# Gate and branch products of a second transformer block computed with tokens on the partitions, with a rearranged merge

## What is computed

```
h = rms_norm(x); z = h @ w_in
zq, zf_f, zf_b, zi, zg, zu, zv, ga, gb = split(z)
a_out = hgrn2_mixer(zq, zf_f, zf_b, zi, zg, ...)      # (256, 1024): two directions, 8 heads of 128
b_out = spatial_gating(zu, zv, ...)                   # (256, 512)
merged = sigmoid(ga) * (a_out @ w_a) + sigmoid(gb) * (b_out @ w_b)
x = x + rms_norm(merged @ w_out)
x = x + rms_norm((silu(h2 @ w_gate) * (h2 @ w_up)) @ w_down)      # h2 = rms_norm(x)
x = x + (p @ w_ple) * sigmoid(x @ w_ple_gate)
```

## Time and profile before

| | |
|---|---|
| three runs | 1087.6, 1088.25, 1090.77 us; median 1088.25 |
| profiled execution | 1089.45 us, its span (first to last instruction) 1087.7 us |
| PE busy | 1074.7 us, 99% of the span |
| DVE, ACT busy | 751.3 us (69%), 602.7 us (55%) |
| HBM read | 180.79 MB, 167 GB/s over the span |
| TensorE clock granted | full throughout |

### The profile page before, as it was taken

One profiled execution on the slowest core, in us unless ns is written; L12 is line 12 of the kernel. 1 busy time (PEld: TensorE's weight loads), 2 busy tenths in 40 slices (PEclk: granted clock), 3 DMA queues, 4 the chain that ended last, 5 costly groups with the idle time before them and its releaser, 6 DMA issues.

```text
span 1087.7 us, 16240 instructions
## 1 busy us (share of the span) xinstructions
PE 1074.7 (99%) x6880; PEld 960.4 (88%) x6880; DVE 751.3 (69%) x897; ACT 602.7 (55%) x731; POOL 0.2 (0%) x4
## 2 busy tenths in 40 slices
PE   9999999999999999999999999999999999999998
PEld 8888777789998988888889899999999888888887
DVE  5465855466745478776568897679947888776557
ACT  5543365543535455555446985589555675554443
POOL 0000000000000000000000000000000000000000
PEclk9999999999999999999999999999999999999999
DMA  9963244565553556564655455443544646664651
GB/s 281 244 215 117 78 155 145 149 209 186 169 188 117 155 184 215 191 194 146 212 182 180 133 156 166 144 156 117 155 155 146 193 155 195 193 194 155 196 172 39
DMA packets 141448, 183.08 MB, mean 168 GB/s; under 512 B 14132, under 2 KB 91936, under 8 KB 141376
## 3 DMA queue, kind: packets, MB, share of 16 engines
q1 hardware_dynamic: 141160, 181.85, 52.8%
q10 hardware_dynamic: 216, 0.21, 0.1%
HBM read 180.79 MB, written 1.25 MB: 167 GB/s over the span
## 4 chain that ended last, share of the span: by engine, by line
PE 91%; ACT 4%; DVE 3%; issue 1%; DVEq 0%; ACTq 0%
PE ps L543 28%; PE ps L569 22%; PE ps L600 14%; PE ps L571 11%; PE ps L987 2%; PE ps L1116 2%; PE ps L646 1%; DVE wlo L1753 1%; PE ps L806 1%; ACT whi L1169 1%; PE ps L781 1%; PE ps L648 1%; PE ps L793 1%; PE ps L876 1%; PE ps L1002 1%
## 5 line engine op out<-in xcount | busy, mean ns | idle before, releaser
L1753 DVE TENSOR_TENSOR wlo<-raw,whi 128x2048 fp32r<-128x2048 f32 (+3 forms) x170 | 378.4, 2228 | 173.1 <-ACT whi L1169 172.6
L1169 ACT ACTIVATE whi<-raw 128x2048 fp32r<-128x2048 f32 (+1 forms) x167 | 310.5, 1863 | 89.9 <-PE ps L571 36.2
L543 PE MATMUL ps<-ha,whi 128*128 128x256 f32 x1328 | 243.1, 285 | 4.3 <-DVE wlo L1753 4.3
L569 PE MATMUL ps<-ha,whi 128*128 128x512 f32 x640 | 226.2, 399 | 0.6 <-DVE wlo L1753 0.6
L543 PEld LDWEIGHTS ps<-ha,whi 128*128 128x128 f32 x1328 | 206.9, 192 | 8.2 <-issue 7.1
L543 PE MATMUL ps<-ha,wlo 128*128 128x256 f32 x664 | 187.8, 283 | 0.0
L571 PE MATMUL ps<-ha,wlo 128*128 128x256 f32 x640 | 179.4, 280 | 0.0
L569 PEld LDWEIGHTS ps<-ha,whi 128*128 128x128 f32 x640 | 120.2, 188 | 30.6 <-issue 0.9
L543 PEld LDWEIGHTS ps<-ha,wlo 128*128 128x128 f32 x664 | 127.2, 192 | 0.0
L569 PE MATMUL ps<-pr,whi 128*128 128x512 f32 x352 | 124.5, 399 | 0.0
L571 PEld LDWEIGHTS ps<-ha,wlo 128*128 128x128 f32 x640 | 120.8, 189 | 0.1
(11 more groups left out here) (381 smaller groups left out, 1691.7 us busy)
## 6 DMA issues: line engine op xcount, KB each, us to landing
raw<-in_w_in SPq DMA_DIRECT2D x54, 1024.0 KB, 5.3
raw<-in_w_ffn_gate SPq DMA_DIRECT2D x11, 1024.0 KB, 5.1
raw<-in_w_ffn_up SPq DMA_DIRECT2D x11, 1024.0 KB, 5.2
raw<-in_w_gate SPq DMA_DIRECT2D x11, 1024.0 KB, 5.1
raw<-in_w_up SPq DMA_DIRECT2D x11, 1024.0 KB, 5.1
raw<-in_w_xkv SPq DMA_DIRECT2D x8, 1024.0 KB, 5.1
raw<-in_w_ffn_down SPq DMA_DIRECT2D x8, 1024.0 KB, 5.0
raw<-in_w_down SPq DMA_DIRECT2D x8, 1024.0 KB, 5.0
```

The source lines that it names most:

```text
L543: mm = e.matmul(ps[0:width, m * T:(m + 1) * T], a[:, kk, m * width:(m + 1) * width], b[:, off + k, :], start=k == 0 and j == 0 and m % 2 = ...
L569: e.matmul(banks[s][:, at_:at_ + 512], wh[:, kk, c], H[2][:, :, k, :], start=k == 0, stop=False, skip_group_check=True)
L1169: e.activation(h, r, ACT.Copy).then_inc(*hi_done.up(n))
L1753: e.tensor_tensor(l, r, h.bitcast(F32), ALU.subtract).then_inc(*lo_done.up(n))
```

## The change

- **Second run of the mixer**: gb0, gb1, wb0, wb1, ga0 and ga1 are computed by `unit_tm` (ten units), and so are the four units of wa0 and wa1. The gates and the merge then have tokens on the partitions.
- **Merge**: each half of `mtmp` is turned back by eight transposes on PE (`turn_merged2`), one group between the two token halves of wa1.1, the other inside `paired` behind its first step; `ml_hi` and `ml_lo` read the turned result in PSUM. On DVE `merged2(1, 0)` comes ahead of `ml_lo(0, 0)`. On ACT the conversion of wa1.1 moves between the two `ao` copies of the second run, and the conversion of wo1 ahead of `ml_hi(0, 0)`.
- **First run of the mixer**: everything on PE from S0 on stands one unit later (S0 behind zu's first unit), and the conversion of zu's first unit stands ahead of the logarithms on ACT and DVE; the slots are renumbered, and `tanh_q(1)` comes ahead of `mix_norm(0)`.
- **Norm behind w_out**: the square and fold of the third piece stand ahead of the conversion of the next unit.
- **Residual**: `add_normed` computes X of tile k+1 ahead of the low part of tile k, in both uses.
- **Start**: the conversion of sq's first unit stands ahead of `rs_tm("mem")`; the masks are loaded behind cc's fetches and converted behind the convolution's taps.

```diff
         fetch_for("fk")
-        e.dma_start(mk[:, :, :], d["c_masks"].rearrange("p (l n) -> p l n", l=7)).then_inc(s_mk, 16)
         fetch_for("fv")
...
-        fetch_for("svf", "sq", "cc", "cu", "cb")
+        fetch_for("svf", "sq", "cc")
+        e.dma_start(mk[:, :, :], d["c_masks"].rearrange("p (l n) -> p l n", l=7)).then_inc(s_mk, 16)
+        fetch_for("cu", "cb")
...
+        def unit_tm(name, i, H, s, free=None, ncol=512, K=8, off=0, ready=None, halves_=False, between=None):
...
             for t in range(2):
+                if t and halves_:
+                    mm.then_inc(*half_done.up((name, 0)))
+                if t and between is not None:
+                    between()
                 for kk in range(nk):
+                    if ready is not None and t == 0 and ready(k) != last_wait:
+                        last_wait = ready(k)
+                        e.wait_ge(*last_wait)
...
-        mixer(0, 1)
-        linear("zu", HA, 0, None, a_stat.on(("ln", "final")), lambda i: mixer(0, 2 + i))
+        linear("zu", HA, 0, None, a_stat.on(("ln", "final")), lambda i: mixer(0, 1 + i))
...
-        linear("gb0", HA, 0, None, a_mix.on(("sig", 1, 1)), lambda i: mixer(1, 1 + i))
...
-        linear("ga1", HA, 1, None, v_evac.on("wb1"), lambda i: mixer(1, 9 + i))
+        for g in range(2):
+            for i in range(2):
+                unit_tm(f"gb{g}", i, HA, g, None if i else (a_mix.on(("sig", 1, 1)), v_mix.on(("zg", 1)))[g])
+                mixer(1, 1 + 2 * g + i)
+        e.wait_ge(*v_split.on("bo"))
+        for g in range(2):
+            unit_tm(f"wb{g}", 0, BO, g, a_stat.on(("tanh", f"gb{g}")), K=4)
+            mixer(1, 5 + g)
+        for g in range(2):
+            for i in range(2):
+                unit_tm(f"ga{g}", i, HA, g, None if i else v_evac.on(f"wb{g}"))
+                mixer(1, 7 + 2 * g + i)
...
+        def turn_merged2(i):
+            e.wait_ge(*v_stat.on(("merged2", i, 1)))
+            for m in range(4):
+                for t_ in range(2):
+                    mm = e.transpose(banks[i][:, m * T + t_ * P:m * T + t_ * P + P],
+                                     mtmp[i][:, 2 * t_ + m // 2, (m % 2) * P:(m % 2) * P + P], ident[:, :])
+                if m % 2:
+                    mm.then_inc(*pe_turn.up(("ml", i, m // 2)))
...
+        unit_tm("wa0", 0, AO, 0, a_stat.on(("tanh", "ga0")), ready=ao_ready)
         mixer(1, 11)
+        unit_tm("wa1", 0, AO, 1, a_stat.on(("tanh", "ga1")), ready=ao_ready)
+        unit_tm("wa0", 1, AO, 0, ready=ao_ready, halves_=True)
+        unit_tm("wa1", 1, AO, 1, halves_=True, between=lambda: turn_merged2(0))
         paired(("wo0", "wo1"), ML, (2, 3), lambda k: v_split.on(("ml", k // 4, k % 4 // 2)),
+               (mix_taken(1, 8, 0), a_mix.on(("ln", 1, 1))), 2, lambda: turn_merged2(1))
...
+        hi(U["svf"][0][0] + 2)
         rs_tm("mem", m_tm, 20)
-        hi_for("svf")
+        hi(U["svf"][1][0] + 2)
...
+                if i == 1 and j == 0:
+                    hi(U["wa1"][1][0])
...
         hi(U["hq0"][1][0] + 2)
+        hi(U["zv"][0][0] + 2)
         half_logs(0, 0)
...
         merged2(0, 1)
+        merged2(1, 0)
         ml_lo(0, 0)
         lo(U["wa1"][1][0] + 2)
+        merged2(1, 1)
         ml_lo(0, 1)
-        merged2(1, 0)
-        merged2(1, 1)
...
+            def added(k):
+                normed(k)
+                e.wait_ge(*v_stat.on(("nh", name, k)))
+                e.tensor_tensor(X[:, k, :], X[:, k, :], nh[:, k, :], ALU.add)
+            added(0)
             for k in range(8):
                 if k < 7:
-                    normed(k + 1)
+                    added(k + 1)
                 e.wait_ge(*v_stat.on((split_name, k)))
...
```

More of the change, by code:

```diff
@@ L588, in both @@
                         between(2 * i + g)
-        def unit_tm(name, i, H, s, free=None, ncol=512, K=8, off=0):
+        def unit_tm(name, i, H, s, free=None, ncol=512, K=8, off=0, ready=None, halves_=False, between=None):
             n, k0, nk = U[name][i]
             wh, wl = weights(n)
+            last_wait = None
             if free is not None:
@@ L629, in column_sums, with paired @@
             mm.then_inc(*pe_sum.up(("sums", name)))
-        def paired(names, H, ss, ready, frees, step=1):
+        def paired(names, H, ss, ready, frees, step=1, middle=None):
             last_wait = None
@@ L651, in paired @@
                         mm.then_inc(*unit_done.up(("unit", n)))
+                if k0 == 0 and middle is not None:
+                    middle()
         def sums_and_ple(name, s, free, i, ps, ready, ple_free):
@@ L1032, in tensor @@
         unit_tm("zv", 1, HA, 3)
-        mixer(0, 1)
-        linear("zu", HA, 0, None, a_stat.on(("ln", "final")), lambda i: mixer(0, 2 + i))
+        linear("zu", HA, 0, None, a_stat.on(("ln", "final")), lambda i: mixer(0, 1 + i))
         for i in range(2):
             unit_tm(f"zi{i}", 0, HA, 1 - i, v_mix.on(("q", 0)) if i == 0 else a_evac.on("zu"))
+            mixer(0, 3 + 2 * i)
+            unit_tm(f"zi{i}", 1, HA, 1 - i)
             mixer(0, 4 + 2 * i)
[L1038 to L1043, removed]
+        linear("zg0", HA, 1, None, a_evac.on(("zi0", 1)), lambda i: mixer(0, 7 + i))
+        linear("hq1", HA, 0, None, a_evac.on(("zi1", 1)), lambda i: mixer(0, 9 + i))
+        unit("ff1", 0, HA, 1, None, v_mix.on(("zg", 0)))
         mixer(0, 11)
-        linear("ff1", HA, 1, None, v_mix.on(("zg", 0)))
+        unit("ff1", 1, HA, 1)
         unit("fb1", 0, HA, 0, None, v_mix.on(("q", 1)))
@@ L1066, in ao_ready @@
         def ao_ready(k):
             return v_split.on(("ao", k // 4, k % 4 // 2))
-        unit("wa0", 0, AO, 0, ao_ready, a_stat.on(("tanh", "ga0")))
+        def turn_merged2(i):
[6 more added lines that the diff above has]
+                    mm.then_inc(*pe_turn.up(("ml", i, m // 2)))
@@ L1082, in tensor @@
         mm.then_inc(*pe_turn.up("p"))
-        piece("wo2", ML, 1, None, v_evac.on(("wa", 1, 1)))
+        piece("wo2", ML, 1, None, v_split.on(("ml", 1, 1)))
         piece("wo3", ML, 2, None, v_evac.on(("mix", 0)), last=True)
@@ L1601, in tanh_zg @@
                 *a_mix.up(("tanh zg", i)))
-        slot(U["zg0"][0][0], 0, 8)
-        hi(U["zg0"][1][0] + 2)
-        mix_scores(0, 8)
+        for k, (u, _, _) in enumerate(U["zg0"]):
+            slot(u, 0, 7 + k)
         tanh_zg(0)
         hi(U["hq1"][0][0] + 2)
-        mix_norm(0)
+        mix_scores(0, 8)
         hi(U["hq1"][1][0] + 2)
@@ L1659, in ml_hi @@
             k0 = 4 * i + 2 * j
-            e.wait_ge(*v_stat.on(("merged2", i, j)))
-            e.activation(ML[0][:, k0:k0 + 2, :], mtmp[i][:, 2 * j:2 * j + 2, :], ACT.Copy,
+            e.wait_ge(*pe_turn.on(("ml", i, j)))
+            e.activation(ML[0][:, k0:k0 + 2, :], wide(banks[i][:, 512 * j:512 * j + 512]), ACT.Copy,
                          scale=0.5).then_inc(*a_split.up(("ml", i, j)))
-        hi(U["wa1"][0][0] + 2)
         hi(U["wa0"][1][0] + 2)
+        hi(U["wa1"][1][0] + 2)
         ml_hi(0, 0)
-        hi(U["wa1"][1][0] + 2)
         ml_hi(0, 1)
@@ L1683, in evac_pieces @@
                 e.activation(mix[:, 2 * g:2 * g + 2, :], split_sums(ss[g])[1], ACT.Copy).then_inc(*a_evac.up((name, g)))
-            before(3)
-            square(4)
+            if square_name == "post mix":
+                square(4)
+                before(3)
+            else:
+                before(3)
+                square(4)
             late()
@@ L1951, in vector @@
                 e.wait_ge(*v_stat.on((f"tap {i}", m)))
+        e.wait_ge(s_mk, 16)
+        e.tensor_copy(masks[:, :, :], mk[:, :, :]).then_inc(*v_stat.up("masks"))
         lo(U["cb"][0][0] + 2)
@@ L2365, in add_pieces @@
             fold_in(1)
-            before(3)
-            fold_in(2)
+            if square_name == "post mix":
+                fold_in(2)
+                before(3)
+            else:
+                before(3)
+                fold_in(2)
             late(0)
@@ L2410, in add_normed @@
                 e.wait_ge(*v_stat.on("x2"))
-            normed(0)
-            for k in range(8):
+            def added(k):
+                normed(k)
                 e.wait_ge(*v_stat.on(("nh", name, k)))
                 e.tensor_tensor(X[:, k, :], X[:, k, :], nh[:, k, :], ALU.add).then_inc(*v_stat.up((split_name, k)))
+            added(0)
+            for k in range(8):
                 if k < 7:
-                    normed(k + 1)
+                    added(k + 1)
                 e.wait_ge(*v_stat.on((split_name, k)))
```

30 lines of the change are left out of this document (11 added, 19 removed).

## The result

Over eight runs of each, measured together, the changed kernel takes 1080.64 us in the median (1077.47 to 1083.71), the kernel before 1088.24 (1085.44 to 1090.94); the ratio is 0.9925, 95% interval 0.9906 to 0.9944, which is 8.2 us less, 6.1 to 10.2. The change is faster, by more than the range allowed. Two executions in the experiments, of 1160.14 and 1167.61 us, ran at a granted clock of 0.85 and are in none of the ratios.

A forecast was written before the change was run, and what follows sets the result against it. PE, busy 99% of the span, was taken to bound the kernel, with DVE the other bound in the mixer's second run. Terms summed to -5.6: 1083.8 against the profiled 1089.45, 1082.6 at the median's level; range 1080.6 to 1086.0.

The forecast's parts named there:

- the range allowed: Whole kernel: forecast range 1080.6 to 1086.0 us, leaving out the slow merge and tails.
- The start: Ahead of sq's first unit: PE's 2.84 us stand goes, sq starts at about 53.3, -2.7.
- `rs_tm`'s rows: Start, within the rival that a gain becomes another wait (0.18): rows 1.9 later are wanted at once, 1.9 goes back.
- First run: First run of the mixer: PE's 0.83 us stall behind S0 goes, -1.1, bounds 0 and -1.3.
- Second run: Second run of the mixer: ten units save 3.0 on PE, DVE lets -1.15 through, bounds 0 and -3.7.
- The sign given: Second run of the mixer: PE's waits in front of the scores grow to 1.5 to 2 us for `am`.
- The rival in which DVE does not bind: Second run: all 3.0 and part of the 0.68 come through, 1080.7 us; chance 0.10.
- Merge: From the sums on: shorter wa units and wait, sixteen transposes, a wait for `merged2(0, 1)`: +0.45, bounds -0.5 and +7.
- the fold: Norm behind w_out: DVE's last fold no longer begins late behind ACT's square, -0.3 before the sums of squares.
- The rival of dear transposes: Merge: at half clock the sixteen transposes take 4.1, 2.5 more than in the sum, 1085.1 us; chance 0.05.
- Norm and residual: `add_normed`: -1.0 behind w_out, bounds +0.15 and -1.9; at the end +0.2 from the later first low part.
- the first step of the sum: Whole kernel: terms summed against the profiled 1089.45 us, the result then taken 1.2 down to the median's level.

The follow-up runs named there:

- the second (10.9, 8.4 to 13.3): Changed kernel measured once more, unedited, beside the kernel before: 1078.03 us in six runs, ratio 0.99 (0.9878 to 0.9923).
- one kernel: Changed kernel with DVE's copy of the transposed `ws` ahead of the low part before it, so au4 finds it done: 1081.1 us, ratio 0.9941.

## Why the prediction was wrong

- **The start**, -2.7: the wait went as forecast, -2.72, and 2.73 when it is undone. What it does to the clock was not in the sum; see below. Neither `rs_tm`'s rows nor the masks were missed.
- **First run**, -1.1: -1.07, alone and in the whole. Right.
- **Second run**, -1.15 of 3.0: -1.18, -1.17 alone. Right, and for the reason given: PE's waits there grew from 0.68 us to 2.13 (0.82, 0.70, 0.61), 1.45 of the 1.8 that did not come through, and 0.93 more came when DVE's slots beside wb were made shorter. The sign given was 1.5 to 2 us of waits for `am`; it was 1.3, and 0.8 for a low part. The rival in which DVE does not bind is excluded.
- **Merge**, +0.45 and -0.3 for the fold: -0.05, alone without the fold +0.27. The transposes took 0.84 and 0.79 from start to start, 1.63 for the 1.6; `merged2(0, 1)` ended at 824.11, 15.5 behind the sums at 808.60, as worked out, and PE waited 0.1 for it where I had 0.25, since it came there at 15.5 itself. The rival of dear transposes is excluded: the sixteen took 1.63, and the granted clock stayed full. The Trainium skill's page "TensorE: Matmul & The Clock Gate", section "Part 4: PE-mode transpose", has some 275 ns for one in a kernel, by which they would take 16 x 0.275 = 4.4, an estimate; the trace does not agree.
- **Norm and residual**, -1.0 and +0.2: -1.06 (the sums to bg1) and +0.16. Right.
- **What failed** is the first step of the sum: that it can be made against one profiled execution, and that its 1.2 us to the median are all that such an execution differs by. Each stage that the change does not touch was put at 0, and the full clock of the one profile was taken for every execution. The runs showed two terms in that place. First, two stages that no edit touches, 300 us long in all, run at one of two paces, 2.6 and 3.3 us apart; before's profiled run had the slow pace in both, after's the fast one in both. Second, the stall that the start edit removes is followed in two thirds of the executions of the kernel before by a fall of the clock to half, 1.5 us each; before's profiled run is of the third without it, so its rows did not show the term. The steps and the second term make 5.9 + 1.0 = 6.9, inside the first measurement (8.2, 6.1 to 10.2) and outside the second (10.9, 8.4 to 13.3). What is left, 1.3 and 4.0, is for the pace, as far as the runs tell, which the changed kernel met in its fast form oftener. The times shown gave a hint that I did not read: 1087.6 to 1090.77 in three runs, a spread of 3.2, as large as the smallest effect that I claimed to tell.

Open is how much oftener the changed kernel meets the fast pace, and why. That it is decided at an interruption is shown for au4 by one kernel. Of the edits ahead of the first part only the start exists; the profiles speak for it (five of five against one of five), the times of its removal are of both kinds. For the second part no single edit is shown to do it.

## What to carry to other kernels

Lay profiles of two kernels side by side by marks also where nothing was edited: here half of the difference between two profiles came from there. Look at the granted clock of every run and not only of the profiled one: a stall can cost more than its length in the executions in which the clock falls behind it, here 2.7 and another 1.5 us. Where an engine runs gapless, the number of its instructions in a window of fixed length shows at once whether it runs at the same pace. And in a stretch with two full engines, a shorter instruction on one is worth only what the other lets through; count what binds from both sides first. Here PE's slots are 7.24 us, and DVE's are 6.99 and, beside wb, 8.1; DVE binds where its chain starts and beside wb, and not in the slots between.

## What was not expected of the hardware

Alternating matmuls of 512 and 256 columns, gapless, at full clock, take 353 or 347 ns a pair, for 139 to 173 us without a change. The rows of equal matmuls beside the mixer showed no such thing: where nothing held it, a unit of 256 columns took 5.84 us and one of 512 took 5.54 (5.57 for the first) in every profile at full clock. The pace changed only where something else stood between the pairs or PE waited, if only 20 ns, and in either direction.

A stall of PE of 2.8 us was followed within 1.4 us by some 3.4 us at half the granted clock in three of five profiles, and not in the other two, with the same instructions on PE around it. It cost 1.5 us each time.
